# Block turns through DRAM and seven-product output projections in the last units of a two-layer encoder

## The reference

```python
pr = sink_softmax(jnp.einsum('bcqkgd,bcskd->bckgqs', qr, kb), sink, valid)
orr = jnp.einsum('bckgqs,bcskd->bcqkgd', pr.astype(v.dtype), vb)
...
scores = jnp.einsum('bcqhd,bcshd->bchqs', q, k) * decay_mask
kv = jnp.einsum('bcshd,hs,bcshe->bchde', k, k_decay, v)
...
mix = jnp.concatenate([y_conv, y_swa, y_ret, y_rwkv], axis=-1) @ w_out[i]
h = layer_norm(ALPHA * h + mix, ln1_g[i], ln1_b[i])
h = layer_norm(ALPHA * h + conv_glu_ffn(h, ffn_w_up[i], ffn_conv_w[i], ffn_w_down[i]), ln2_g[i], ln2_b[i])
```

## Time and profile before

| | |
|---|---|
| runs of the kernel before | median 3052.5 us (3052.41 to 3058.36, 3 runs) |
| the profiled execution | 3056.32 us, its span 3054.4 us |
| granted TensorE clock | 0.999 |
| busy | TensorE 3011.8 us, VectorE 1529.4, ScalarE 939.6, POOL 216.8 |
| DMA | 760.19 MB, mean 249 GB/s |

### The profile page before, as it was taken

The page is one execution under the profiler, slowest core; times in us unless marked ns, Lnnn a source line. Parts: engine busy times, 40 slices in busy tenths (PEclk is TensorE's granted clock), DMA queues, the critical chain, the costliest instruction groups (busy, mean ns, idle before and its releaser), DMA issues.

```text
span 3054.4 us, 64343 instructions
## 1 busy us (share of the span) xinstructions
PE 3011.8 (99%) x27180; PEld 2759.9 (90%) x27180; DVE 1529.4 (50%) x3672; ACT 939.6 (31%) x2381; POOL 216.8 (7%) x319
## 2 busy tenths in 40 slices
PE   8999999999999999999999999999999999999998
PEld 7788778889898899989989899999999999999998
DVE  4345552355633455336554366544566255663562
ACT  3324440134421343124341144303343043421320
POOL 0111010011101110010010101000000000000000
PEclk9999999999999999999999999999999999999999
DMA  7577477788978989888797898986768857787887
GB/s 256 170 205 213 118 208 218 220 237 283 311 236 263 280 273 320 242 259 272 238 313 210 264 276 261 295 284 196 260 205 268 290 178 249 210 267 253 301 302 248
DMA packets 227116, 760.19 MB, mean 249 GB/s; under 512 B 25088, under 2 KB 44672, under 8 KB 226576
## 3 DMA queue, kind: packets, MB, share of 16 engines
q1 hardware_dynamic: 189328, 620.80, 61.6%
q0 software_dynamic: 37504, 135.28, 18.0%
HBM read 744.33 MB, written 136.31 MB: 288 GB/s over the span
## 4 chain that ended last, share of the span: by engine, by line
PE 92%; DMA 3%; DVE 3%; ACT 2%; issue 0%; SPq 0%; ACTq 0%; DVEq 0%
PE psum L1853 29%; PE psum L1306 27%; PE psum L1876 10%; PE psum L1912 8%; PE psum L1443 7%; DMA slots<-in_weights 2%; PE psum L1300 1%; PE psum L1322 1%; PE psum L1621 1%; PE psum L1646 1%; DMA slots<-wsum 1%; PE psum L1633 1%; PE psum L1572 1%; PE psum L1694 1%; PE psum L1803 1%
## 5 line engine op out<-in xcount | busy, mean ns | idle before, releaser
L1306 PE MATMUL psum<-hT,slots 128*128 128x256 f32 (+1 forms) x2880 | 658.9, 387 | 2.8 <-ACT hT L874 2.1
L1306 PEld LDWEIGHTS psum<-hT,slots 128*128 128x128 f32 x2880 | 541.6, 190 | 97.0 <-issue 5.5
L1853 PE MATMUL psum<-tsum,slots 128*128 128x128 f32 (+1 forms) x4928 | 608.0, 277 | 11.6 <-ACT raw L1223 4.9
L1853 PEld LDWEIGHTS psum<-tsum,slots 128*128 128x128 f32 x4928 | 573.1, 191 | 28.6 <-issue 20.2
L1853 PE MATMUL psum<-hT,slots 128*128 128x128 f32 (+1 forms) x3696 | 453.7, 276 | 6.9 <-DMA slots<-in_weights 3.9
L1853 PEld LDWEIGHTS psum<-hT,slots 128*128 128x128 f32 x3696 | 432.6, 192 | 10.1 <-DMA slots<-in_weights 4.9
L1876 PE MATMUL psum<-gT,slots 128*128 128x256 f32 (+1 forms) x1408 | 309.9, 383 | 0.0
L1876 PEld LDWEIGHTS psum<-gT,slots 128*128 128x128 f32 x1408 | 267.1, 190 | 40.9
L1306 PE MATMUL psum<-mixT,slots 128*128 128x256 f32 (+2 forms) x1024 | 226.4, 381 | 1.1 <-DVE hT L2030 1.1
L1306 PEld LDWEIGHTS psum<-mixT,slots 128*128 128x128 f32 x1024 | 194.3, 190 | 29.7 <-issue 1.5
L2030 DVE SCALAR_TENSOR_TENSOR hT<-hT,psum 128x256 f32<-128x256 f32 (+2 forms) x96 | 40.5, 423 | 348.3 <-PE psum L1876 249.7
(11 more groups left out here) (326 smaller groups left out, 3526.6 us busy)
## 6 DMA issues: line engine op xcount, KB each, us to landing
slots<-in_weights SPq DMA_DIRECT2D x667, 512.0 KB, 4.6
slots<-wsum SPq DMA_DIRECT2D x308, 512.0 KB, 4.5
wsum<-in_weights POOLq DMA_DIRECT2D x132, 512.0 KB, 6.7
slots<-wsumi SPq DMA_DIRECT2D x64, 512.0 KB, 4.4
slots<-wsumd SPq DMA_DIRECT2D x64, 512.0 KB, 4.5
wsum<-wsum POOLq DMA_DIRECT2D x44, 512.0 KB, 7.9
wsumi<-in_weights POOLq DMA_DIRECT2D x24, 512.0 KB, 7.5
wsumd<-in_weights POOLq DMA_DIRECT2D x24, 512.0 KB, 9.3
```

What stands on the lines that cost most here:

```text
L1306: ins = mm(psum[:, i % 2, :n], lhsT, rhs, start=k == 0, stop=k == len(pairs) - 1)
L1853: ins = mm(dst[:, e * n:(e + 1) * n], w[:, (4 * e + k) * P:(4 * e + k + 1) * P], moving[s][k], start=s in (0, 1, 5) and e == 0 and k == 0, ...
```

## The change

In units 5 to 7 (`KEYS_FROM = 5`) the four transposes of keys and values per tile are gone from TensorE: VectorE turns 32 by 32 blocks of both tiles in one instruction (`cut_keys`, in the input projection), SP writes them to DRAM (512 KB) behind block `is3_2` and reads them back in token order with four DMAs behind `is3_5`. In units 6 and 7 (`WEIGHTS_FROM = 6`) the attention weights go the same way: two block transposes by VectorE per tile, one write (512 KB), four reads (two behind each of two neighbouring up blocks). The product with the values comes five lane steps later than it did, and the second tile's attention five steps later. The writes and reads stand in SP's list ahead of the slot load of that place.

In units 5 and 6 (`OUT_FAST`) the output projection is done by seven products, 14 blocks `os0_0` to `os1_6`, with sums of the mixed features in `tsum` (`mix_sums`, during the down-projection before). The weight of the output projection is stored by quadrants, so in the other units two slots are taken for two blocks. POOL makes the eight quadrant sums `wsumo` with 16 DMAs (`out_sums`). The ring for POOL's DMAs is halved, and the semaphores of the down sums become one.

```diff
+OUT_FAST = [5, 6]
...
+def out_names(u):
+
+    return [f"os{g}_{s}" for g in range(2) for s in range(7)] if u in OUT_FAST else [f"out{m}" for m in range(KD)]
...
+KEYS_FROM, WEIGHTS_FROM = 5, 6
...
+VALUES_STEP, PUT_AFTER, GET_AFTER = 9, 4, 10
...
+def out_spare():
+
+    return [i for i, (u, name) in enumerate(BLOCKS) if (u == 2 and name[:2] in ("dn", "ds")) or (u == NCH and name in MIX_PART)]
...
+            m = int(name[3:])
+            if m % 2 == 0:
+                out += [(l, N_IN + m + half, u, f"out{m + 1}", None) for half in range(2)]
...
+            def keys_to_dram(u):
+
+                sp.wait_ge(S["cut"], keys_cut(u) + 1)
+                if keys_cut(u):
+                    sp.wait_ge(S["cut_in"], 64 * keys_cut(u))
+                sp.dma_start(kvdram, kvcut).then_inc(S["cut_out"], 16)
+
+            def keys_by_tokens(u):
+
+                sp.wait_ge(S["cut_out"], 16 * (keys_cut(u) + 1))
+                source = kvdram.rearrange("(q s) (i b c) -> b s i q c", q=4, i=2, b=4)
+                for b in range(4):
+                    here = slice(BLOCK * b, BLOCK * (b + 1))
+                    sp.dma_start(kvturned[here].rearrange("p i q r s -> p i q (r s)"), source[b]).then_inc(S["cut_in"], 16)
+
+            def weights_to_dram(nth):
+
+                sp.wait_ge(S["cut"], nth + 1)
+                sp.wait_ge(S["cut_in"], 64 * nth)
+                sp.dma_start(pdram, sc[:, 0:1024]).then_inc(S["cut_out"], 16)
+
+            def weights_by_keys(nth, half):
+
+                sp.wait_ge(S["cut_out"], 16 * (nth + 1))
+                source = pdram.rearrange("(b s) (q c) -> q s b c", b=4, q=4)
+                for q in (2 * half, 2 * half + 1):
+                    sp.dma_start(PB[BLOCK * q:BLOCK * (q + 1)].rearrange("p b m c -> p b (m c)"), source[q]).then_inc(S["cut_in"], 16)
...
+                    if name0[:2] == "us" and AT[u0, name0] in turns:
+                        what, *which_turn = turns[AT[u0, name0]]
+                        (weights_to_dram if what == "put" else weights_by_keys)(*which_turn)
+                    if u0 >= KEYS_FROM and name0 == "is3_2":
+                        keys_to_dram(u0)
+                    if u0 >= KEYS_FROM and name0 == "is3_5":
+                        keys_by_tokens(u0)
...
+                for group in range(2):
+                    for kind, first in (("S1", "A21"), ("S3", "A11"), ("S2", "A11"), ("S4", "A12")):
+                        yield in_time()
+                        g.dma_start(out_block(kind, group), out_block(first, group), max_dma_last_dim=4096).then_inc(S["wo_made"], 16)
+                for kind, more, count in (("S1", "A22", 128), ("S3", "A21", 128), ("S2", "S1", 192), ("S4", "S2", 224)):
+                    for group in range(2):
+                        yield in_time()
+                        g.wait_ge(S["wo_made"], count)
+                        g.dma_start(out_block(kind, group), out_block(more, group), accum_op=ALU.add,
+                                    max_dma_last_dim=4096).then_inc(S["wo_made"], 16)
...
+                if u == NCH - 1:
+                    sums_until(4, first_up)
...
+                    if not keys_by_blocks(u, j):
+                        for ct in range(2):
...
+                    if weights_by_blocks(u, j):
+                        for _ in range(VALUES_STEP - 3):
+                            yield
+                        pe.wait_ge(S["cut_in"], 64 * (weights_cut(u, nth) + 1))
+                        for m in range(2):
+                            rows_m = min(w - P * m, P)
+                            for kv in range(2):
+                                ins = mm(bank(BX)[HD * kv:HD * kv + HD, 0:2 * P].rearrange("p (b c) -> p b c", b=4),
+                                         Vw[:rows_m, b, m, HD * kv:HD * kv + HD],
+                                         PB[:rows_m, :, m, 2 * BLOCK * kv:2 * BLOCK * (kv + 1)], start=m == 0, stop=m == 1)
+                        ins.then_inc(S["a_oT"], 1)
+                        yield
+                        continue
...
-                for m in range(KD):
-                    rest(dense(u, f"out{m}", [mixT[:, k, first:n] for k in range(KD)]))
-                    if 0 < u < NU - 1 and m == 0:
-                        ln_mean(2 * u - 1)
-                    if 0 < u < NU - 1 and m == 4:
-                        ln_var(2 * u - 1)
+                if u in OUT_FAST:
+                    out_by_seven(u, [mixT[:, k, first:n] for k in range(KD)])
+                    return
...
+                for g in range(2):
+                    base = AT[u, f"os{g}_0"]
+                    for s in range(7):
+                        w = next_slot()
+                        bank_free(base + s)
+                        if (g, s) == (0, 1):
+                            pe.wait_ge(S["osum"], 4 * (OUT_FAST.index(u) + 1))
+                        dst = product_at(u, base, s)
+                        for e in range(2):
+                            for k in range(4):
+                                ins = mm(dst[:, e * n:(e + 1) * n], w[:, (4 * e + k) * P:(4 * e + k + 1) * P], moving[s][k],
+                                         start=s in (0, 1, 5) and e == 0 and k == 0, stop=k == 3, skip_group_check=True)
+                        ins.then_inc(S["blk"], 1)
+                        if (g, s) == (0, 1):
+                            ln_mean(2 * u - 1)
+                        if (g, s) == (1, 5):
+                            ln_var(2 * u - 1)
...
+            def mix_sums(u):
+
+                first, n = span_of(u, 0)[0] - chunk_of(u)[0], span_of(u, 0)[1]
+                h, before = n // 2, 4 * OUT_FAST.index(u)
+                b11, b12 = (mixT[:, 0:4, first + h * i:first + h * (i + 1)] for i in range(2))
+                b21, b22 = (mixT[:, 4:8, first + h * i:first + h * (i + 1)] for i in range(2))
+                t1, t3, t2, t4 = (tsum[:, j, :, :h] for j in range(4))
+                v.wait_ge(S["conv"], 2 * u + 2)
+                v.wait_ge(S["w_mix"], 2 * u + 2)
+                v.wait_ge(S["r_mix"], u + 1)
+                v.wait_ge(S["a_mix"], tiles_before(u) + len(tiles_of(u)))
+                v.wait_ge(S["blk"], AT[u - 1, up_names(u - 1)[-1]] + 1)
+                tt(t1, b11, b12, ALU.subtract).then_inc(S["osum"], 1)
+                tt(t3, b22, b12, ALU.subtract).then_inc(S["osum"], 1)
+                v.wait_ge(S["osum"], before + 2)
+                stt(t2, t3, -1.0, b11, ALU.mult, ALU.subtract).then_inc(S["osum"], 1)
+                v.wait_ge(S["osum"], before + 3)
+                stt(t4, t2, -1.0, b21, ALU.mult, ALU.subtract).then_inc(S["osum"], 1)
...
+            def cut_keys(u):
+
...
+                r = ROW["rk0"]
+                v.transpose(kvcut.rearrange("p (c r s) -> p c r s", c=8, r=4),
+                            rows[:, r:r + 4, 2:2 + 2 * P].rearrange("p r (c s) -> p c r s", c=8)
+                            ).then_inc(S["cut"], 1)
...
+                        after(step(ins))
+                        for m in range(2):
+                            ins = v.transpose(PC[:, 0:4 - m, m].rearrange("p q (h s) -> p q h s", h=4),
+                                              PR[:, :, P * m:P * m + P - BLOCK * m].rearrange("p h (q s) -> p q h s", s=BLOCK))
+                        ins.then_inc(S["cut"], 1)
+                        for _ in range(VALUES_STEP - 4):
+                            yield
...
+                if u in OUT_FAST:
+                    for g in range(2):
+                        for s in range(7):
+                            out_step(u, g, s)
+                            if g or s > 1:
+                                advance(program, 1)
+                    rest(program)
+                    return
...
-    nc = bacc.Bacc("TRN2", target_bir_lowering=False, num_devices=1, dynamic_dma_scratch_size=2048)
+    nc = bacc.Bacc("TRN2", target_bir_lowering=False, num_devices=1, dynamic_dma_scratch_size=1024)
```

More of the change, by code:

```diff
@@ L124, with keys_by_blocks, weights_by_blocks, tiles_where @@
 SWA_PART = ["sq0", "sq1", "sk", "sv"]
+def keys_by_blocks(u, j):
+    return u >= KEYS_FROM and j > 0
+def weights_by_blocks(u, j):
+    return u >= WEIGHTS_FROM and j > 0
+def tiles_where(test, nth):
+    return sum(test(*tile) for tile in ALL_TILES[:nth])
+def keys_cut(u):
+    return u - KEYS_FROM + tiles_where(weights_by_blocks, tiles_before(u))
+def weights_cut(u, nth):
+    return u + 1 - KEYS_FROM + tiles_where(weights_by_blocks, nth)
+def tiles_not(test, nth):
+    return nth - tiles_where(test, nth)
 def input_part(u):
@@ L2704, in down @@
                         residual(u, DOWN_ENDS[q], 1)
+                    if u + 1 in OUT_FAST and q == 20:
+                        mix_sums(u + 1)
                     if u == NU - 2 and q in DOWN_ENDS and DOWN_ENDS[q] == 0:
```

178 lines of the change are left out of this document (137 added, 41 removed).

## The result

| | changed kernel | kernel before |
|---|---|---|
| median of the runs | 3088.1 us (3085.23 to 3090.35, 4 runs) | 3054.94 us (3052.41 to 3058.36, 4 runs) |
| ratio | 1.0107 [1.0091, 1.0123] | |
| profiled execution, its span | 3090.35 us, 3088.6 us | 3056.32 us, 3054.4 us |
| granted TensorE clock | 0.993 | 0.999 |

The forecast was 3073 us, slower. The kernel is slower, and by 14 us more than the sum gave: the spans are 34.2 us apart where it gave 20.4.

What follows compares the result with a forecast made beforehand. TensorE, busy 3011.8 of 3054.4 us, was taken to bound the kernel. Gains of -11.8, mask wait +27, clock +2, normalisation +2.2 and SP +1 gave +20.4 us on 3052.5, so 3073 us, with bounds 3062 to 3088.

Steps and rivals of the forecast that it cites:

- the sum: Whole kernel: -11.8 + 27 + 2 + 2.2 + 1 = +20.4 us, slower, giving 3073 us.
- TensorE's gains, 11.8 us: TensorE: output projections 5.2 us less, key and value transposes 2.9, attention-weight transposes 3.7; bounds 11 to 12.5.
- The wait for the masks: TensorE waits for unit 4's rwkv-lane masks from 1468.05 to 1495, 27 us; bounds 20 to 34.
- POOL's chain: POOL ahead of the masks: eight copies 23.3 us, four accumulations 10 + 3, then two, then two; masks at 1495.
- What it loses there it waits less for the masks: Stretch ahead of the mask wait: contention slows TensorE, but the wait shortens by as much, so nothing was added.
- The clock, 2 us: Behind the mask wait TensorE's clock must come back: 2 us added, bounds 1.4 and 4.
- Normalisation, 1.1 us twice: Output projections of units 5 and 6: late scalings make TensorE wait 1.1 us each, 2.2 us; bounds 0 to 4.
- T: End of the last output block; the forecast had ScalarE's scalings end at T + 7.8.
- SP, 1 us: SP's list: key turns delay slot loads 0.3 us in each of three units, weight turns nothing; together 1 us.
- No wait: Rival: POOL's burst costs TensorE nothing visible; -8.6 us, 3044 us; chance 0.06.
- small wait: Rival: copies go far faster, TensorE waits about 5 us for the masks; -3.6 us, 3049 us; chance 0.07.
- SP as a brake: Rival: key turns hold slots 3 us each, weight turns 1.25; 14 us in place of 1, 3086 us; chance 0.07.

Runs made afterwards that it cites:

- turns_alone: Changed kernel with plain output projections everywhere and no output sums; turns through DRAM and half ring stay: 3050.92 us, ratio 0.9985 to the kernel before.
- masks_first: Changed kernel with the 16 output-sum DMAs behind unit 4's masks and the first down sums in POOL's list: 3045.96 us, ratio 0.9975 to the kernel before.
- out_alone_ring: Changed kernel without the turns, with POOL's DMA ring back at 2048: 3089.37 us, ratio 1.0115 to the kernel before.
- half_ring: Kernel before with only POOL's DMA ring halved, 2048 to 1024: 3049.62 us, ratio 0.9988.
- single: pairs_alone with one slot for each plain output block again: 3052.4 us, ratio 0.9993 to the kernel before.
- best: Changed kernel: output sums behind masks, earlier variance and reciprocal (units 5, 6), one slot per plain output block, down sums on two semaphores; 3045.02 us, ratio 0.9963.
- out_alone: Changed kernel without the turns; seven-product output projections, output sums ahead of the masks and half ring stay: 3088.86 us, ratio 1.0111 to the kernel before.
- pairs_alone: Changed kernel without turns, seven-product projections and output sums; slot pairs, one semaphore and half ring stay: 3059.16 us, ratio 1.0005 to the kernel before.

## Why the prediction was right, and where its sizes were off

The forecast had the sign, the place of the loss and its cause. It had the size only just: the forecast's own bounds ended at 3088 us and the median is 3088.1. The wait, 35.1 us, lies above its bound of 34, and gains that the sum didn't have, the half ring's above all, made up for part of that. That the total still fell at the edge is luck in part.

- **TensorE's gains, 11.8 us: right.** out(5) and out(6) -2.62 and -2.63 (forecast 2.6 each). The turns gave 3.12 and 2.97 us in up(5) and up(6) of turns_alone (2.84 each). In the changed kernel itself these stages are only 1.46 and 2.47 us shorter; a slot wait of 1.41 us stands in its up(5). The 0.98 us of up(4) can't be seen among its slot waits.
- **The wait for the masks: right mechanism, too small.** masks_first shows the cause by removing it. The mis-sized term is POOL's chain: 35.1 us of wait for 27. Step by step in out_alone_ring: the copies were through after 28.5 us (23.3, and 1 for what was left of the sums ahead), the four accumulations took 17.3 (13), the next two 8.2 (9). Of the copies' 28.5 us some belong to the sums ahead: POOL's queue moved 4.8 MB in that time, the eight copies are 4.2. The slot loads moved 6.6 MB beside them, 232 GB/s, where they had 200 beside the 13 copies of the earlier trace rows; I read the slower copies from that, no run tests it. The accumulations are the clearer miss. The forecast had them at 4.8 us each beside slot loads and at half of that, 2.4, alone; no row stood behind the half, and alone they took 4.3. On top came a step that the forecast put at nothing without a reason: it named the halved ring in the change and gave it no cost, and POOL's wait for it is worth 3.2 us at the masks.
- **"What it loses there it waits less for the masks": right, and it hides part of the miss.** From the start of up(3) TensorE came to L1777 2.8 us later than before (1472.1 less 1445.83, against 1468.05 less 1444.55) and waited that much less. Both together, the masks released TensorE 37.9 us later than it had asked for them before, 10.9 more than the 27 of the forecast.
- **The clock, 2 us: right.** 26.60 us behind the end of the stall TensorE stood where it stood 23.96 us behind 1468.05 before: 2.6 us. The granted clock was 0.50 up to 1513.
- **Normalisation, 1.1 us twice: right mechanism, 0.77 and 0.78 measured**, and gone when the variance came earlier. ScalarE's scalings ended 7.8 us behind T, as worked out.
- **SP, 1 us: right for the turns.** The changed kernel shows no wait behind a turn, the others at most 0.3 to 1.5 us behind unit 5's key turn and 0.8 behind one weight turn. But out(4), in(5) and up(4) together took 5.9 us more, in slot waits. The forecast's bounds for this term add up to 3 x 3 + 4 x 1.25 = 14 us, and the upper end of its sum took 5.
- **A gain that the sum didn't have:** the half ring takes 4.7 us from up(3) in half_ring (2 to 6 over the kernels compared there).
- **The rivals.** No wait, small wait and SP as a brake are all refuted. The rule of the Trainium skill by which the wait would be 5 us (DMA: Bandwidth & Descriptors, Anatomy of one DMA) gave 3049 us; the copies ran at a third of its pace, beside the slots' traffic.

The 13.8 us that the sum missed are: 8.1 in the wait, 2.8 ahead of it, 0.6 clock, -4.7 ring, 6.9 in out(4) to up(4) (5.9, and 1.0 of gain that doesn't show), -0.7 normalisation, -1.0 SP, 1.3 that lie ahead of up(3), where the change does nothing; 13.3 together, the rest being small waits and gains that partly cancel.

**What stays open.** Why in(5) and up(4) took 88.6 to 91.6 and 180.6 to 186.0 us in nearly all kernels made from the changed one, against 87.8 and 179.4 to 179.9 before and with the half ring. Turns, pairs and ring are each cleared as the sole cause, the one semaphore may account for 2 us. The profiles don't line up behind ring and semaphore together either: single has both and 88.74 and 183.35 us, the one semaphore by itself gives 89.02 and 181.70, and best, with two semaphores and the half ring, 89.32 and 181.20. The one pair that differs in the ring alone is out_alone, with 91.59 and 181.09, and out_alone_ring, with 87.82 and 180.64, the one kernel of these whose in(5) is as short as before. The DMA share is 0.88 to 0.95 over in(5), not the 1.03 that the expectation of pairs_alone names, and 0.98 to 1.01 in the 20 to 30 us of up(4) in which most of the waits lie. Executions of one kernel lie up to 11 us apart (3050.83 to 3062.06 for pairs_alone), and one profile for each kernel doesn't settle a matter of 3 us. Where in DRAM the new buffers lie wasn't tried. Nor is it known why an accumulation that waits on the semaphore which its neighbours raise is held until one has landed, though the count is reached.

## What to carry to other kernels

Before bulk DMAs are bound to a place in an engine's list, look at what small work stands behind them in the same list and who waits for it: 16 DMAs that cost TensorE 1 us (in one kernel some 5) behind three 0.3 us masks cost it 35 us ahead of them. A binding to block numbers spreads nothing when the list comes to it late; the first of the 16 was bound to a block of down(2), which begins at 1248.91, and went out at 1446.86 with all the others behind it. And seven products for eight trade TensorE's time for loads: count the DMA share of the stage first. With plain blocks out(5) stood at 0.64, went to 0.89 and gained 2.6 us; out(4) stood at 0.99 and lost 5.9 (29.20 to 35.11).

## What the runs showed of the hardware that I had not expected

- With the ring at 1024 POOL has seven copies of 384 or 512 KB or three accumulations outstanding and then stands itself for some 13 to 19 us; at 2048 it issued 13 copies, or six accumulations on semaphores of their own, without a wait. This throttle was worth 4.7 us to TensorE in half_ring and cost it 3.1 us of wait in out_alone.
- Four accumulations took 17 us with TensorE idle and no slot loads (window of the stall: 141 GB/s, DMA share 0.64), 4.3 us each: so their pace isn't one of contention with the slots alone.
- The down sums' accumulations on one shared semaphore were issued 1, 2, 3 (half ring) or 1, 5 (full ring), with 6.4 to 11.8 us between, where separate semaphores gave 3, 3 and 6. The four of the output sums, on a shared semaphore too, went out 3, 1 with either ring, 8.5 to 12.7 us between.
